# A chunked delta rule with chunks of 128 tokens in place of 64

## The chip, the cores and the metric

The kernel runs on one core of one Trainium2 chip. The time is that of the device, in microseconds (us), from the start of the program to its end. TensorE (PE in the profile) multiplies matrices, VectorE (DVE), ScalarE (ACT) and GpSimd (POOL) work element by element, SyncE (SP) issues transfers. The engines run their own instruction streams in order and meet at semaphores.

## What is computed

Two layers, one after the other, on a sequence of 1024 tokens of width 1024. The change lies in one part of the second layer, the gated delta rule with 4 heads of width 128. The reference computes it by chunks; here CHUNK is 64 and dk = dv = 128:

```python
gc = jnp.cumsum(g.reshape(b, h, n, CHUNK), axis=-1)
diff = gc[..., :, None] - gc[..., None, :]
decay = jnp.exp(jnp.where(tril_incl, diff, -jnp.inf))
kb = kc * bc[..., None]
a_mat = jnp.where(tril_strict, jnp.einsum('bhnid,bhnjd->bhnij', kb, kc) * decay, 0.0)
l_mat = a_mat + jnp.eye(CHUNK)
u = triangular_solve(l_mat, vc * bc[..., None])
w = triangular_solve(l_mat, kb * jnp.exp(gc)[..., None])
attn_intra = jnp.einsum('bhnid,bhnjd->bhnij', qc, kc) * decay
...
def step(state, inp):                       # scanned over the chunks
    v_new = u_i - w_i @ state
    o_i = qd_i @ state + a_i @ v_new
    state = state * gl_i + kt_i.T @ v_new
```

The recurrence S_t = exp(g_t)(I - beta_t k_t k_t^T) S_(t-1) + beta_t k_t v_t^T does not depend on how the tokens are cut into chunks, so a kernel may choose another chunk.

## The kernel before, in words

The kernel is a row of stages, each with its own block of instructions and a barrier behind it. The stage in question is `stage_delta` (L1559), between the projections of the second layer and `stage_causal`. Its input (q, k and v, turned, for all tokens) lies in SBUF already. Only the gate's constants and three masks are loaded.

The 1024 tokens are 8 tiles of 128. All 4 heads are done in one step: a step of TensorE is 4 matmuls of 128 columns (the trace counts 8 records, two for each float32 matmul; transposes have one) into one PSUM bank of 512 columns, and VectorE, ScalarE or GpSimd then handle 128x512 elements in one instruction. Three things are done for each tile:

- **front** (L1644): decays, the gram matrix of k, the product with q, the matrix A = strict lower part of the gram matrix times the decays, and the first level of the inverse, T (and X, its transpose). With CHUNK 64 the masks `upper`, `strict` and `levels` leave two blocks of 64x64 in each 128x128 matrix.
- **inv** (L1696): the inverse of the unit triangle by doubling. Level l joins blocks of 2^l to blocks of 2^(l+1). A level is a fixed loop over three engines: `z` (TensorE, Z = Al X, L1708), a copy of Z from PSUM (ScalarE, L1984), `update` (TensorE, dX = T Z at L1719 and dT = Z T at L1723), then X - dX (L1862) and T - dT (L1865) on VectorE. The next `z` waits for both (L1702, L1703). The last level needs no dT. Level 0 is done in the front, levels 1 to 5 here. `apply` (L1727) then makes u and w.
- **rec** (L1738): the recurrence. `read` (L1740) multiplies w and q with the state S, VectorE makes v_new (L1880); `write` (L1757) makes the update of S and the product of attention and v_new; VectorE adds the update to the decayed state (L1887), which GpSimd has made (L2098). A chunk has one read and one write, a tile of 128 tokens has two of each, with 64 rows in them.

The order of all engines is written out by `order` (L1612). Round i runs the front of tile i, the inverse of tile i-1 and the recurrence of tile i-2, dovetailed by levels: between `z` and `update` of a level stands a piece of the front, and behind `update` of levels 1 to 4 stands a read or a write. Rounds 0 and 1 have no recurrence, round 0 no inverse, round 8 has no front, round 9 only the recurrence. Rounds 2 to 7 have all three.

Of the kernel before, what the change touches and what calls it, by code (L numbers as in the profile page):

```python
# [42 lines left out]

D_IN2 = 4104
DN_HEADS, DK = 4, 128
CHUNK = 64
Z2, BA2, AQ2, AK2, AV2, AG2 = 1536, 2048, 2056, 2568, 3080, 3592
ATT_HEADS = 8
DILATION = (1, 4, 16)
STEPS = (P, P, P)  # L50
LEVELS = 6
CW = 256


# [1504 lines left out]
def stage_delta(nc, g):  # L1559
# [7 lines left out]
    with ExitStack() as ctx:  # L1567
# [10 lines left out]
        tl = k.sb("d_tl", [P, 12])  # L1578
        etl = k.sb("d_etl", [P, 3, 12])
# [63 lines left out]
        def _(pe):  # L1643
# [93 lines left out]

            class rec:  # L1738
                @staticmethod
                def read(t, c):  # L1740

                    n = 2 * t + c
                    r = slice(c * CHUNK, (c + 1) * CHUNK)
                    pe.wait_ge(s["w_copied"], t + 1)
                    if n >= 1:
                        pe.wait_ge(s["S_ready"], n)
                    if c == 0 and t >= 1:
                        pe.wait_ge(s["oq_ready"], t)
                    for h in range(H4):
                        last = nc.tensor.matmul(bank(6)[r, h, :], wT[:, t % 2, h, r], S[:, h, :], start=True, stop=True)  # L1750
                    last.then_inc(s["wS_ready"], 1)
                    for h in range(H4):
                        last = nc.tensor.matmul(bank(7)[r, h, :], g.qT[:, h, t * P + c * CHUNK:t * P + (c + 1) * CHUNK],
                                                S[:, h, :], start=True, stop=True)

                @staticmethod
                def write(t, c):  # L1757

                    n = 2 * t + c
                    r = slice(c * CHUNK, (c + 1) * CHUNK)  # L1760
                    pe.wait_ge(s["vnew_ready"], n + 1)
                    if c == 0 and t >= 1:
# [23 lines left out]
        def _(dve):  # L1786
# [6 lines left out]
            class front:  # L1793
                @staticmethod
                def first(t):
                    dve.wait_ge(s["gcb_ready"], t + 1)
                    if t >= 1:
                        dve.wait_ge(s["decays_done"], t)
                    for h in range(H4):

                        nc.vector.tensor_scalar(dd[:, 0, h, :], bank(0)[:, h, :], gc[:, t, h:h + 1], 0.0,
                                                ALU.subtract, ALU.max)
                        nc.vector.tensor_scalar(dd[:, 1, h, :], bank(0)[:, h, :], gc[:, t, h:h + 1], 0.0,
                                                ALU.subtract, ALU.min)
                    for c in range(2):
                        r = slice(c * CHUNK, (c + 1) * CHUNK)
# [31 lines left out]
                @staticmethod  # L1838
                def attn(t):
                    dve.wait_ge(s["attn_ready"], t + 1)  # L1840
                    dve.wait_ge(s["decT_masked"], t + 1)
                    if t >= 3:
                        dve.wait_ge(s["av_ready"], 2 * (t - 2))
# [26 lines left out]

            class rec:
                @staticmethod
                def read(t, c):
                    n = 2 * t + c
                    r = slice(c * CHUNK, (c + 1) * CHUNK)
                    dve.wait_ge(s["wS_ready"], n + 1)
                    dve.wait_ge(s["u_copied"], t + 1)
                    if n >= 2:
                        dve.wait_ge(s["av_ready"], n - 1)
                    nc.vector.tensor_tensor(vnew[r, :, :], u[r, t % 2, :, :], bank(6)[r, :, :], ALU.subtract).then_inc(s["vnew_ready"], 1)  # L1880

                @staticmethod
                def write(t, c):
                    n = 2 * t + c
                    dve.wait_ge(s["dS_ready"], n + 1)
                    dve.wait_ge(s["Sg_ready"], n + 1)
                    nc.vector.tensor_tensor(S[:, :, :], Sg[:, :, :], bank(6), ALU.add).then_inc(s["S_ready"], 1)  # L1887

                @staticmethod
                def finish(t):  # L1890
                    dve.wait_ge(s["av_ready"], 2 * t + 2)
# [42 lines left out]
        def _(act):  # L1934
            class front:
                @staticmethod
                def first(t):
# [4 lines left out]
                        act.wait_ge(s["dec_masked"], t)  # L1942
                        act.wait_ge(s["decT_masked"], t)
                    if t >= 3:
                        act.wait_ge(s["Sg_ready"], 2 * (t - 2))
# [30 lines left out]
            class inv:  # L1976
# [13 lines left out]
                @staticmethod  # L1990
                def apply(t):
                    if t >= 2:
                        act.wait_ge(s["vnew_ready"], 2 * (t - 1))
                    act.wait_ge(s["u_ready"], t + 1)
                    nc.scalar.copy(u[:, t % 2, :, :], bank(3)).then_inc(s["u_copied"], 1)
                    if t >= 2:
                        act.wait_ge(s["wS_ready"], 2 * (t - 1))
                    act.wait_ge(s["w_ready"], t + 1)
                    nc.scalar.copy(wT[:, t % 2, :, :], bank(4)).then_inc(s["w_copied"], 1)

            class rec:
                @staticmethod
                def read(t, c):
                    pass

                @staticmethod
# [1 line left out]
                    pass  # L2008

                @staticmethod  # L2010
                def write(t, c):
# [15 lines left out]
        def _(pool):  # L2027
# [6 lines left out]
            class front:  # L2034
# [13 lines left out]
                def khat_turn(t):  # L2048
# [2 lines left out]
                        pool.wait_ge(s["w_ready"], t - 1)  # L2051
                    nc.gpsimd.tensor_tensor(kbe[:, t % 2, :, :], khat[:, :, :], per_row(be[:, t, :]), ALU.mult).then_inc(s["kbe_ready"], 1)
                    if t >= 3:
                        pool.wait_ge(s["dS_ready"], 2 * (t - 2))
# [34 lines left out]

            class rec:  # L2090
                @staticmethod
                def read(t, c):

                    n = 2 * t + c
                    if n >= 1:
                        pool.wait_ge(s["S_ready"], n)
                    decay = etl[:, t % 3, 4:12].rearrange("p (h c) -> p h c", c=2)[:, :, c]
# [3 lines left out]
                def write(t, c):  # L2101
                    if c == 0 and t >= 1:
                        square(t - 1)

                @staticmethod
# [645 lines left out]
```

## Time and profile before

| | us |
|---|---|
| median of 3 runs | 1763.53 (1762.84 to 1763.92) |
| profiled execution | 1763.42 |
| its span in the profile | 1761.6 |
| delta stage, first to last matmul | 1216.9 to 1480.0 |
| a round with front, inverse and recurrence | 29.90 |

The page gives each engine's busy time over the whole span. The stage is read from the rows in order of time, further below: each has the start, the time, the line and operation, the count of records, and in brackets how long the engine sat idle before and for whom. A time from one start to the next start holds the idle time too, and is what the sums go by.

### The profile page before, as it was taken

The page shows a single profiled execution, that of the slowest core. Times are in us where ns is not written, and L with a number is a line of the kernel's source. Part 1 is how long each engine was busy: PE and PEld are TensorE (multiplying, and loading weights), DVE is VectorE, ACT ScalarE, POOL GpSimd, SP SyncE. Part 2 cuts the span into 40 slices and gives each one's busy share as a digit, 9 for nine tenths or more (in the row PEclk, how much of TensorE's full clock was granted, in tenths as well). Part 3 has the DMA queues.
Part 4 walks back from the last instruction along what each step waited for, and adds up shares of the span by engine and source line. Part 5 has one row for each costly group of instructions (what it writes and reads, how often), then busy time and mean ns, then how long its engine had stood idle before and what let it go on. Part 6 is the DMA issues. An engine that isn't in the chain of part 4 may idle for free. (4 is left out here: it accounts for less than half of the span.)

```text
span 1761.6 us, 27770 instructions
## 1 busy us (share of the span) xinstructions
PE 1632.9 (93%) x11048; PEld 1465.0 (83%) x11048; DVE 887.5 (50%) x1668; ACT 598.5 (34%) x1171; POOL 449.3 (26%) x508
## 2 busy tenths in 40 slices
PE   6999999799997998899999999996899997899799
PEld 6998899678876997678999988895788886899687
DVE  5339100588886997244041544342455553677431
ACT  5231011377774563233221223232212111566300
POOL 0212211000003562330122222212555541332320
PEclk9999999899998999899999999998999998999899
DMA  7312112000002111652142552201000002211242
GB/s 223 67 58 87 47 55 73 20 1 1 1 1 79 55 37 29 184 165 85 24 50 73 94 68 55 48 29 34 1 1 1 1 1 90 67 49 37 74 143 73
DMA packets 78454, 100.33 MB, mean 57 GB/s; under 512 B 20559, under 2 KB 63311, under 8 KB 78328
## 3 DMA queue, kind: packets, MB, share of 16 engines
q1 hardware_dynamic: 78328, 98.57, 21.2%
q8 instruction: 89, 1.46, 0.3%
q14 instruction: 37, 0.30, 0.1%
HBM read 75.45 MB, written 23.11 MB: 56 GB/s over the span
## 5 line engine op out<-in xcount | busy, mean ns | idle before, releaser
L301 POOL TENSOR_TENSOR p_w_lo<-p_w_raw,p_w_hi 128x2048 fp32r<-128x2048 f32 (+1 forms) x27 | 126.9, 4699 | 554.1 <-ACT p_w_hi L296 554.1
L332 PE MATMUL op_ps<-p_w_hi,w_out_hi 128*128 128x256 f32 (+1 forms) x640 | 182.1, 284 | 0.4 <-ACT p_spill L357 0.4
L332 PE MATMUL op_ps<-p_w_hi,w_out_lo 128*128 128x256 f32 (+1 forms) x640 | 179.7, 281 | 0.0
L332 PE MATMUL op_ps<-p_w_lo,w_out_hi 128*128 128x256 f32 (+1 forms) x640 | 179.6, 281 | 0.0
L332 PE MATMUL p_ps<-p_w_hi,hT_hi 128*128 128x256 f32 x576 | 163.5, 284 | 0.0
L332 PE MATMUL p_ps<-p_w_lo,hT_hi 128*128 128x256 f32 x576 | 162.8, 283 | 0.0
L332 PE MATMUL p_ps<-p_w_hi,hT_lo 128*128 128x256 f32 x576 | 162.8, 283 | 0.0
L332 PEld LDWEIGHTS op_ps<-p_w_hi,w_out_hi 128*128 128x128 f32 x640 | 120.6, 188 | 1.5 <-ACT p_spill L357 0.8
L332 PEld LDWEIGHTS op_ps<-p_w_lo,w_out_hi 128*128 128x128 f32 x640 | 120.8, 189 | 0.0
L332 PEld LDWEIGHTS op_ps<-p_w_hi,w_out_lo 128*128 128x128 f32 x640 | 120.6, 188 | 0.0
L296 ACT CAST p_w_hi<-p_w_raw 128x2048 fp32r<-128x2048 f32 (+1 forms) x29 | 55.3, 1908 | 167.5 <-DMA p_w_raw<-w_in 89.0
L332 PEld LDWEIGHTS p_ps<-p_w_lo,hT_hi 128*128 128x128 f32 x576 | 109.3, 190 | 0.0
L332 PEld LDWEIGHTS p_ps<-p_w_hi,hT_hi 128*128 128x128 f32 x576 | 109.3, 190 | 0.0
L332 PEld LDWEIGHTS p_ps<-p_w_hi,hT_lo 128*128 128x128 f32 x576 | 109.2, 190 | 0.0
L746 DVE TENSOR_TENSOR a_pt_lo<-a_ps,a_pt_hi 128x512 fp32r<-128x512 f32 x128 | 82.3, 684 | 24.1 <-ACT a_pt_hi L806 24.1
L806 ACT CAST a_pt_hi<-a_ps 128x512 fp32r<-128x512 f32 x128 | 68.8, 590 | 54.6 <-PE a_ps L670 54.5
L741 DVE TENSOR_REDUCE a_stat<-a_ps 128x1 f32<-128x1024 f32 x64 | 77.7, 1214 | 2.2 <-PE a_ps L660 2.2
L2296 PE MATMUL c_ps<-c_v,c_prob_t 128*128 128x128 f32 x576 | 76.2, 279 | 0.0
L332 PE MATMUL op_ps<-w_out_hi,p_w_hi 128*128 128x512 f32 x192 | 76.1, 396 | 0.0
L941 PEld LDWEIGHTS b_ps<-b_v,b_prob_t 128*128 128x128 f32 x544 | 70.0, 191 | 7.2 <-issue 1.6
L332 PE MATMUL op_ps<-w_out_hi,p_w_lo 128*128 128x512 f32 x192 | 75.7, 394 | 0.0
L332 PE MATMUL op_ps<-w_out_lo,p_w_hi 128*128 128x512 f32 x192 | 75.5, 393 | 0.0
(291 smaller groups left out, 4063.4 us busy)
## 6 DMA issues: line engine op xcount, KB each, us to landing
p_w_raw<-w_in SPq DMA_DIRECT2D x28, 1024.0 KB, 8.3
s_gate<-p_spill SPq DMA_DIRECT2D x48, 128.0 KB, 1.8
kbT<-x SPq DMA_DIRECT2D x8, 512.0 KB, 5.9
b_w_raw<-w_out SPq DMA_DIRECT2D x8, 512.0 KB, 5.4
qT<-s_gate SPq DMA_DIRECT2D x8, 512.0 KB, 5.5
qT<-x SPq DMA_DIRECT2D x8, 512.0 KB, 3.6
s_x<-qT SPq DMA_DIRECT2D x8, 512.0 KB, 2.6
c_table<-s_line SPq DMA_DIRECT2D x8, 512.0 KB, 4.0
```

What stands on the lines that cost most here:

```text
L296: self.nc.scalar.copy(self.w_hi[:, c % 2, :, 0:w], self.raw[:, :, 0:w]).then_inc(self.w_hi_ready, 1)
L301: ops.tensor_tensor(self.w_lo[:, c % 2, :, 0:w], self.raw[:, :, 0:w], self.w_hi[:, c % 2, :, 0:w].bitcast(F32), ALU.subtract).then_inc(sel ...
L332: last = self.nc.tensor.matmul(out, lhs, rhs, start=(kt == 0 and i == 0), stop=(kt == KT - 1 and i == 2))
L741: nc.vector.tensor_reduce(stat[:, 0, u:u + 1], s, AX.X, ALU.max, negate=True).then_inc(max_ready, 1)
L746: nc.vector.tensor_tensor(part(pt_lo, grp, half, i), ps[:, 4 + half, :].rearrange("p (c q) -> p c q", c=4), part(pt_hi, grp, half, i).bitc ...
L806: nc.scalar.copy(part(pt_hi, grp, half, i), ps[:, 4 + half, :].rearrange("p (c q) -> p c q", c=4)).then_inc(pt_hi_ready, 1)
L941: last = nc.tensor.matmul(ps[:, 6 + u % 2, 0:P], prob_t[:, u % 2, j * P:(j + 1) * P], v[:, t0 + j, p * P:(p + 1) * P], start=(j == 0), sto ...
L2296: last = nc.tensor.matmul(ps[:, 6 + u % 2, 0:P], prob_t[:, u % 3, j * P:(j + 1) * P], v[:, j, pair * P:(pair + 1) * P], start=(j == 0), st ...
```

## The change

`CHUNK` becomes 128 and `LEVELS` 7. A tile is one chunk: its triangle is a full 128x128 one, which takes a level more, and there is one read and one write of the state for a tile. The read stands behind level 2 and the write behind level 4. The recurrence's matmuls have 128 rows in place of 64. The end-of-chunk decays `tl` are one column for each head, which makes one small VectorE instruction less for each tile.

```diff
-CHUNK = 64
+CHUNK = 128
-LEVELS = 6
+LEVELS = 7
...
@@ order
-                if f and l >= 2:
+                if f and 2 <= l <= 5:
                     (front.khat_turn, front.gram, front.attn, front.x0)[l - 2](i)
                 if v:
                     inv.update(i - 1, l)
                 if f and l == 1:
                     front.khat(i)
-                if r and l <= 4:
-                    (rec.read, rec.write)[(l - 1) % 2](i - 2, (l - 1) // 2)
+                if r and l == 2:
+                    rec.read(i - 2)
+                if r and l == 4:
+                    rec.write(i - 2)
...
@@ tensor, rec
                     for h in range(H4):
-                        last = nc.tensor.matmul(bank(6)[r, h, :], wT[:, t % 2, h, r], S[:, h, :], start=True, stop=True)
+                        last = nc.tensor.matmul(bank(6)[:, h, :], wT[:, t % 2, h, :], S[:, h, :], start=True, stop=True)
...
-                        last = nc.tensor.matmul(bank(6)[:, h, :], ktail[r, t % 3, h, :], vnew[r, h, :], start=True, stop=True)
+                        last = nc.tensor.matmul(bank(6)[:, h, :], ktail[:, t % 3, h, :], vnew[:, h, :], start=True, stop=True)
...
-                        last = nc.tensor.matmul(bank(5)[r, h, :], attnT[r, t % 3, h, r], vnew[r, h, :], start=True, stop=True)
+                        last = nc.tensor.matmul(bank(5)[:, h, :], attnT[:, t % 3, h, :], vnew[:, h, :], start=True, stop=True)
...
@@ vector, front.first
-                    for c in range(2):
-                        r = slice(c * CHUNK, (c + 1) * CHUNK)
-                        nc.vector.tensor_tensor(tl[r, 0:H4], bank(0)[r, :, (c + 1) * CHUNK - 1], gc[r, t, :], ALU.subtract)
-                    ends = bank(0).rearrange("p h (c j) -> p h c j", c=2)[:, :, :, CHUNK - 1]
-                    nc.vector.tensor_copy(tl[:, 4:12].rearrange("p (h c) -> p h c", c=2), ends).then_inc(s["diffs_done"], 1)
+                    nc.vector.tensor_tensor(tl[:, 0:H4], bank(0)[:, :, CHUNK - 1], gc[:, t, :], ALU.subtract)
+                    nc.vector.tensor_copy(tl[:, H4:2 * H4], bank(0)[:, :, CHUNK - 1]).then_inc(s["diffs_done"], 1)
```

The other lines of the diff carry the same through: waits that counted 2 t + c count t, slices `[r, ...]` become whole tiles, the masks come out of `CHUNK` and `LEVELS`.

TensorE in a round with all three parts, before, from the `update` of level 1 on. L1719 and L1723 are the update, L1708 is z, L1750/L1753 the read, L1765/L1768 the write, L1670 a transpose of the front.

```order
L1719 MATMUL d_ps<-d_Z,d_T 128x128 x4
L1723 MATMUL d_ps<-d_T,d_Z 128x128 x4
L1750 MATMUL d_ps<-d_S,d_wT 64x128 x4
L1753 MATMUL d_ps<-d_S,qT 64x128 x4
L1708 MATMUL d_ps<-d_X,d_Al 128x128 x4
L1670 MATMUL d_ps<-ident,d_khat 128x128 x4
L1719 MATMUL d_ps<-d_Z,d_T 128x128 x4
L1723 MATMUL d_ps<-d_T,d_Z 128x128 x4
L1765 MATMUL d_ps<-d_vnew,d_ktail 128x128 x4
L1768 MATMUL d_ps<-d_vnew,d_attnT 64x128 x4
```

The same place after the change (L1721 and L1725 are the update, L1710 z, L1749/L1752 the read, L1672 and L1680 pieces of the front):

```order
L1721 MATMUL d_ps<-d_Z,d_T 128x128 x4
L1725 MATMUL d_ps<-d_T,d_Z 128x128 x4
L1710 MATMUL d_ps<-d_X,d_Al 128x128 x4
L1672 MATMUL d_ps<-ident,d_khat 128x128 x4
L1721 MATMUL d_ps<-d_Z,d_T 128x128 x4
L1725 MATMUL d_ps<-d_T,d_Z 128x128 x4
L1749 MATMUL d_ps<-d_S,d_wT 128x128 x4
L1752 MATMUL d_ps<-d_S,qT 128x128 x4
L1710 MATMUL d_ps<-d_X,d_Al 128x128 x4
L1680 MATMUL d_ps<-d_khatT 128x128 x4
```

Behind the update of level 1 z now follows directly; the read stands behind the update of level 2, with 128x128 outputs, and behind the update of level 3 z follows directly again.

TensorE at the end of the inverse, before, from z of level 5 on (L1693 is a transpose of the front, L1732/L1735 are `apply`):

```order
L1708 MATMUL d_ps<-d_X,d_Al 128x128 x4
L1693 MATMUL d_ps<-ident,d_T 128x128 x4
L1719 MATMUL d_ps<-d_Z,d_T 128x128 x4
L1732 MATMUL d_ps<-d_vb,d_X 128x128 x4
L1735 MATMUL d_ps<-d_X,d_kbe 128x128 x4
L1708 MATMUL d_ps<-d_X,d_Al 128x128 x4
```

and after (L1695 is that transpose, L1734/L1737 are `apply`):

```order
L1710 MATMUL d_ps<-d_X,d_Al 128x128 x4
L1695 MATMUL d_ps<-ident,d_T 128x128 x4
L1721 MATMUL d_ps<-d_Z,d_T 128x128 x4
L1725 MATMUL d_ps<-d_T,d_Z 128x128 x4
L1710 MATMUL d_ps<-d_X,d_Al 128x128 x4
L1721 MATMUL d_ps<-d_Z,d_T 128x128 x4
L1734 MATMUL d_ps<-d_vb,d_X 128x128 x4
L1737 MATMUL d_ps<-d_X,d_kbe 128x128 x4
L1710 MATMUL d_ps<-d_X,d_Al 128x128 x4
```

The update of level 5 now has its second half, and a z and a first half of an update, level 6, come behind it with nothing in between.

## Rows read from the trace of the kernel before

**Rows 1.** Busy time by stretch: stretch, length, engines, PEclk, DMA share, GB/s.
```profile
1352.50:1382.40 29.90, 28.61 (x232) 26.36 (x233) 16.48 (x32) 6.33 (x12) 16.40 (x14) 1.00 0.00 1
...
1232.00:1236.00 4.00, 2.64 (x11) 2.24 (x12) 0.63 (x1) 0.58 (x1) 4.00 (x4) 0.51 0.00 2
...
1248.00:1253.00 5.00, 4.02 (x36) 3.86 (x36) 2.07 (x3) 0.59 (x1) 2.88 (x3) 1.00 0.02 3
```

**Rows 2.** TensorE in order of time, repeating tile: start, us, line, operation, count, idle before.
```profile
1336.92 1.10 PE L1719 MATMUL d_ps<-d_Z,d_T 128*128 128x128 f32 x8
...
1340.73 1.16 PE L1708 MATMUL d_ps<-d_X,d_Al 128*128 128x128 f32 x8
...
1342.62 1.10 PE L1719 MATMUL d_ps<-d_Z,d_T 128*128 128x128 f32 x8
...
1344.55 1.16 PE L1765 MATMUL d_ps<-d_vnew,d_ktail 64*128 64x128 f32 x8
...
1346.65 1.16 PE L1708 MATMUL d_ps<-d_X,d_Al 128*128 128x128 f32 x8
...
1348.48 1.16 PE L1719 MATMUL d_ps<-d_Z,d_T 128*128 128x128 f32 x8 [0.24 <-ACT d_Z L1984]
1350.42 1.16 PE L1732 MATMUL d_ps<-d_vb,d_X 128*128 128x128 f32 x8 [0.78 <-DVE d_X L1862]
...
1352.51 1.13 PE L1708 MATMUL d_ps<-d_X,d_Al 128*128 128x128 f32 x8
...
1355.24 1.06 PE L1719 MATMUL d_ps<-d_Z,d_T 128*128 128x128 f32 x8
...
1357.12 1.09 PE L1750 MATMUL d_ps<-d_S,d_wT 128*64 128x128 f32 x8
...
1359.02 1.16 PE L1708 MATMUL d_ps<-d_X,d_Al 128*128 128x128 f32 x8
...
1412.31 1.13 PE L1708 MATMUL d_ps<-d_X,d_Al 128*128 128x128 f32 x8
```

**Rows 3.** TensorE in order of time, before and in the first tile's inverse.
```profile
1216.93 0.61 PE L1778 MATMUL d_ps<-d_g,d_upper 128*128 128x32 f32 x2 [10.02 <-DVE d_g L1920]
...
1244.25 1.16 PE L1719 MATMUL d_ps<-d_Z,d_T 128*128 128x128 f32 x8 [0.24 <-ACT d_Z L1984]
...
1247.29 1.13 PE L1708 MATMUL d_ps<-d_X,d_Al 128*128 128x128 f32 x8 [0.98 <-DVE d_T L1865]
...
1249.15 1.10 PE L1719 MATMUL d_ps<-d_Z,d_T 128*128 128x128 f32 x8
...
1252.13 1.13 PE L1708 MATMUL d_ps<-d_X,d_Al 128*128 128x128 f32 x8 [0.98 <-DVE d_T L1865]
```

**Rows 4.** VectorE in order of time, first tile and then repeating tile.
```profile
1246.34 0.69 DVE L1865 TENSOR_TENSOR d_T<-d_T,d_ps 128x512 f32<-128x512 f32 x1 [0.20 <-PE d_ps L1723]
...
1356.65 0.32 DVE L1807 TENSOR_TENSOR d_tl<-d_ps,d_gc 64x4 f32<-64x4 f32 x2
1356.98 0.17 DVE L1809 COPY d_tl<-d_ps 128x8 f32<-128x8 f32 x1
...
1357.79 0.68 DVE L1865 TENSOR_TENSOR d_T<-d_T,d_ps 128x512 f32<-128x512 f32 x1
```

**Rows 5.** TensorE in order of time, last inverse and last recurrence.
```profile
1442.21 1.13 PE L1708 MATMUL d_ps<-d_X,d_Al 128*128 128x128 f32 x8
1444.02 1.16 PE L1719 MATMUL d_ps<-d_Z,d_T 128*128 128x128 f32 x8 [0.68 <-ACT d_Z L1984]
...
1447.89 1.16 PE L1708 MATMUL d_ps<-d_X,d_Al 128*128 128x128 f32 x8
...
1471.98 1.09 PE L1750 MATMUL d_ps<-d_S,d_wT 128*64 128x128 f32 x8 [0.73 <-ACT d_wT L1999]
...
1475.97 1.09 PE L1750 MATMUL d_ps<-d_S,d_wT 128*64 128x128 f32 x8
```

**Rows 6.** DMA issues at the stage's start: KB each, us to landing.
```profile
d_levels<-c_levels SPq DMA_DIRECT2D x1, 384.0 KB, 3.2
```

More of the change, by code:

```diff
@@ L1577, in stage_delta @@
         dec = k.sb("d_dec", [P, 2, H4, P])
-        tl = k.sb("d_tl", [P, 12])
-        etl = k.sb("d_etl", [P, 3, 12])
+        tl = k.sb("d_tl", [P, 8])
+        etl = k.sb("d_etl", [P, 3, 8])
         khat = k.sb("d_khat", [P, H4, P])
@@ L1739, in read, with write @@
                 @staticmethod
-                def read(t, c):
-                    n = 2 * t + c
-                    r = slice(c * CHUNK, (c + 1) * CHUNK)
+                def read(t):
                     pe.wait_ge(s["w_copied"], t + 1)
-                    if n >= 1:
-                        pe.wait_ge(s["S_ready"], n)
-                    if c == 0 and t >= 1:
+                    if t >= 1:
+                        pe.wait_ge(s["S_ready"], t)
                         pe.wait_ge(s["oq_ready"], t)
                     for h in range(H4):
-                        last = nc.tensor.matmul(bank(6)[r, h, :], wT[:, t % 2, h, r], S[:, h, :], start=True, stop=True)
+                        last = nc.tensor.matmul(bank(6)[:, h, :], wT[:, t % 2, h, :], S[:, h, :], start=True, stop=True)
                     last.then_inc(s["wS_ready"], 1)
                     for h in range(H4):
-                        last = nc.tensor.matmul(bank(7)[r, h, :], g.qT[:, h, t * P + c * CHUNK:t * P + (c + 1) * CHUNK],
+                        last = nc.tensor.matmul(bank(7)[:, h, :], g.qT[:, h, t * P:(t + 1) * P],
                                                 S[:, h, :], start=True, stop=True)
                 @staticmethod
[L1757 to L1762, printed above, removed]
+                def write(t):
+                    pe.wait_ge(s["vnew_ready"], t + 1)
+                    if t >= 1:
                         pe.wait_ge(s["o_ready"], t)
                     for h in range(H4):
-                        last = nc.tensor.matmul(bank(6)[:, h, :], ktail[r, t % 3, h, :], vnew[r, h, :], start=True, stop=True)
+                        last = nc.tensor.matmul(bank(6)[:, h, :], ktail[:, t % 3, h, :], vnew[:, h, :], start=True, stop=True)
                     last.then_inc(s["dS_ready"], 1)
                     for h in range(H4):
-                        last = nc.tensor.matmul(bank(5)[r, h, :], attnT[r, t % 3, h, r], vnew[r, h, :], start=True, stop=True)
+                        last = nc.tensor.matmul(bank(5)[:, h, :], attnT[:, t % 3, h, :], vnew[:, h, :], start=True, stop=True)
                     last.then_inc(s["av_ready"], 1)
@@ L1842, in attn @@
                     if t >= 3:
-                        dve.wait_ge(s["av_ready"], 2 * (t - 2))
+                        dve.wait_ge(s["av_ready"], t - 2)
                     nc.vector.tensor_tensor(attnT[:, t % 3, :, :], bank(0), dec[:, 1, :, :], ALU.mult).then_inc(s["attnT_ready"], 1)
@@ L1872, in read, with write @@
                 @staticmethod
[L1873 to L1876, printed above, removed]
+                def read(t):
+                    dve.wait_ge(s["wS_ready"], t + 1)
                     dve.wait_ge(s["u_copied"], t + 1)
-                    if n >= 2:
-                        dve.wait_ge(s["av_ready"], n - 1)
-                    nc.vector.tensor_tensor(vnew[r, :, :], u[r, t % 2, :, :], bank(6)[r, :, :], ALU.subtract).then_inc(s["vnew_ready"], 1)
+                    if t >= 1:
+                        dve.wait_ge(s["av_ready"], t)
+                    nc.vector.tensor_tensor(vnew[:, :, :], u[:, t % 2, :, :], bank(6), ALU.subtract).then_inc(s["vnew_ready"], 1)
                 @staticmethod
[L1883 to L1886, printed above, removed]
+                def write(t):
+                    dve.wait_ge(s["dS_ready"], t + 1)
+                    dve.wait_ge(s["Sg_ready"], t + 1)
                     nc.vector.tensor_tensor(S[:, :, :], Sg[:, :, :], bank(6), ALU.add).then_inc(s["S_ready"], 1)
@@ L1890, in finish @@
                 def finish(t):
-                    dve.wait_ge(s["av_ready"], 2 * t + 2)
+                    dve.wait_ge(s["av_ready"], t + 1)
                     if t >= 1:
@@ L1944, in first @@
                     if t >= 3:
-                        act.wait_ge(s["Sg_ready"], 2 * (t - 2))
+                        act.wait_ge(s["Sg_ready"], t - 2)
                     nc.scalar.activation(dec[:, 0, :, :], dd[:, 0, :, :], ACT.Exp, scale=-1.0)
@@ L1992, in apply @@
                     if t >= 2:
-                        act.wait_ge(s["vnew_ready"], 2 * (t - 1))
+                        act.wait_ge(s["vnew_ready"], t - 1)
                     act.wait_ge(s["u_ready"], t + 1)
@@ L1996, in apply @@
                     if t >= 2:
-                        act.wait_ge(s["wS_ready"], 2 * (t - 1))
+                        act.wait_ge(s["wS_ready"], t - 1)
                     act.wait_ge(s["w_ready"], t + 1)
@@ L2002, in read @@
                 @staticmethod
-                def read(t, c):
+                def read(t):
                     pass
@@ L2010, in write @@
                 @staticmethod
-                def write(t, c):
+                def write(t):
                     pass
@@ L2091, in read, with write @@
                 @staticmethod
[L2092 to L2097, printed above, removed]
+                def read(t):
+                    if t >= 1:
+                        pool.wait_ge(s["S_ready"], t)
+                    decay = etl[:, t % 3, H4:2 * H4]
                     nc.gpsimd.tensor_tensor(Sg[:, :, :], S[:, :, :], per_row(decay), ALU.mult).then_inc(s["Sg_ready"], 1)
                 @staticmethod
-                def write(t, c):
-                    if c == 0 and t >= 1:
+                def write(t):
+                    if t >= 1:
                         square(t - 1)
```

3 lines of the change are left out of this document (1 added, 2 removed).

## The prediction

> **What bounds the kernel now.** I read the busy times by stretch first. In a repeating stretch of the delta stage, 29.90 us long, TensorE is busy 28.61 us, VectorE 16.48, GpSimd 16.40 and ScalarE 6.33, at a granted clock of 1.00 [rows 1]. So TensorE sets the pace there, and the others have over 13 us to spare in each round. Next I read TensorE in order of time. z of level 1 starts at 1352.51 and, two rounds later, at 1412.31, which is twice 29.90: the rounds repeat [rows 2]. The reader should see in these rows that TensorE hardly waits (0.24 and 0.78 us where a bracket stands), although each level is a loop over three engines. It doesn't wait because other work lies in the two places of a level where it could: a piece of the front between z and the update, a read or write of the state between the update and the next z.
>
> That cover is what I ask about, because the change takes half of it away. Two stretches show a level without it. In round 1, which has no recurrence, z starts 0.98 us after TensorE fell idle, waiting for T of VectorE [rows 3]. In round 8, which has no front, the update waits 0.68 us for the copy of Z [rows 5]. I count from start to start, since such a distance holds work and wait together.
>
> **What a covered and a bare turn take.** From the start of an update to the start of the next z:
> - with a read behind it: 1355.24 to 1359.02, 3.78 us, and 1336.92 to 1340.73, 3.81 [rows 2]
> - with a write behind it: 1342.62 to 1346.65, 4.03 [rows 2]
> - bare: 1249.15 to 1252.13, 2.98, and 1244.25 to 1247.29, 3.04 [rows 3]
>
> So a read or write of about 2 us that is taken out gives only 0.8 to 1.0 us. The rest of it was cover.
>
> **Round with all three parts (6 of them, rounds 2 to 7).**
> - Level 1: the read goes. z of level 2 then waits for T. VectorE first has the decay differences and the small `tl` instructions in its queue, so T starts at 1357.79 and ends at 1358.47 [rows 4]. The change has one L1807 less (two took 0.32), so T ends 0.16 earlier, at 1358.31. From the end of T (1246.34 + 0.69 = 1247.03 [rows 4]) to z (1247.29 [rows 3]) are 0.26 us, so z starts at 1358.57, that is 3.33 after the update in place of 3.78: -0.45.
> - Level 2: a write goes, the read comes in. The write takes 2.10 (1344.55 to 1346.65), a read with 64 rows 1.90 (1357.12 to 1359.02) [rows 2]. A read or write with 128 rows stands in no row. The nearest thing is an update, two steps of full width: 1.88 (1355.24 to 1357.12) and 1.93 (1342.62 to 1344.55) [rows 2]. I take 1.90, with 1.88 and 2.10 as ends: -0.20.
> - Level 3: the read goes, bare turn: 3.81 to 2.98, -0.83.
> - Level 4: the write stays, with 128 rows: 2.10 to 1.90, -0.20.
> - Level 5: was the last level, and its update led to `apply` 1.94 us later (1348.48 to 1350.42 [rows 2]). That distance now belongs to level 6. In its place comes an update with both halves and a bare turn: +3.04.
> - Level 6: z and a bare wait for the copy of Z: 1442.21 to 1444.02, +1.81 [rows 5].
>
> Sum: -1.68 + 4.85 = +3.17 us for a round, 29.90 to 33.07. Six rounds: +19.0.
>
> The Trainium skill, in TensorEngine Tiling (Array Packing), section Key Properties, says that changing the tiling mode drains TensorE; by that the 64-row matmuls cost twice, once on the way in and once on the way out, and the change would gain where they go. The trace has 0.20 us more for a write than for a read, which may be such a drain, and none at a read, which at 1.90 equals a full-width pair [rows 2]. If the rule charged reads too, the read that stays would be 0.20 shorter in each tile, 1.6 us in all, and the sum 1784 in place of 1785.7.
>
> **The other rounds.** Round 1 has no recurrence to take out: +4.85 for the level, -0.16 for `tl`: +4.7. Round 8 has no front: level 1 was 3.87 with its read (1444.02 to 1447.89 [rows 5]) and becomes a bare turn of 3.04, -0.83; level 3 the same; levels 2 and 4 -0.20 each; the new level +4.85: +2.8. Round 9 is recurrence alone, where nothing was cover: one read and one write go, 1471.98 to 1475.97, -3.99 [rows 5], and the write that stays is -0.20: -4.2. Round 0: the smaller `tl` stands ahead of the chain, -0.2.
>
> **What costs nothing, and what hides it.** GpSimd makes one mask product more for a tile and one decayed state less, both 128x512, with 13.5 us idle in a round [rows 1]. The masks are made a round before they are used. Its one decayed state now stands behind `read` at level 2, ahead of the masks, and VectorE wants it only at level 4. The square of the outputs moves behind the masks, and VectorE sums it at the round's end. VectorE has one X and one T more and one v_new and one S less for a tile; X, T and v_new of level 2 fall in its idle time. ScalarE has one more copy of Z, in its idle 23 us. The mask load grows from 384 to 448 KB, from 3.2 us [rows 6] to some 3.7 by size; TensorE waits until 1216.93 for the gates anyway, 10.02 us long [rows 3], so 0, and 0.5 at most. The read of a tile needs the state of the tile before, which is written a round earlier in both kernels.
>
> **Sum.** 19.0 + 4.7 + 2.8 - 4.2 - 0.2 = +22.1 us, for which the levels pay 8 x 4.85 = 38.8 and the recurrence gives back 16.7. The profiled execution took 1763.42 (span 1761.6), 0.1 below the median of 1763.53. So 1785.6, and 1785.7 against the median.
>
> Ends: 16 reads and writes at 1.88 in place of 1.90 give -0.3, at 2.10 +3.2. All bare turns at 2.98, level 1 too, give 6 x 0.35 + 8 x 0.06 + 2 x 0.06, -2.7. All at 3.33 give 6 x 0.35 + 8 x 0.29 + 2 x 0.29, +5.0. With the masks' 0.5 the forecast's own range is 1782.7 to 1794.4.
>
> **Rivals.**
> 1. *TensorE's work decides, and the turns are covered after all* (faster). Counted in steps the change is good: of a round with all parts it takes a read and a write (1.90 + 2.10) and 0.20 from the write that stays, and adds three steps (z, half an update at level 5, half an update at level 6) of 0.95, half of 1.90, 2.9 in all: -1.3. Rounds 2 to 8 -9.1, round 1 +2.9, round 9 -4.2: -10.4, or 1753. For it: 28.61 busy of 29.90, so the stage looks bound by TensorE's busy time [rows 1]. Against it: the bare turns, which show where time goes when the cover goes [rows 3, 5]; nothing else stands in TensorE's queue to fill them, since the order is fixed. It decides if a turn without cover costs under a third of what these rows have: +22.1 is -10.4 plus 32.5 us of new waits. Chance 6 in 100.
> 2. *The clock falls in the new waits* (much slower). The head of the stage, after long waits, ran at 0.51, that is 1.2 GHz [rows 1]. A round's 28.6 us of busy TensorE would take up to as much again: with one round so it is 1814, with all eight near 2000. Against it: the stretch 1248 to 1253, with the same bare turns and TensorE busy 4.02 of 5.00, has 1.00, that is 2.4 GHz [rows 1]. The new rounds are denser than that. The Trainium skill, in TensorE: Matmul & The Clock Gate, section Loop structure matters more than you think, warns that waits between matmuls let the engine go cold; what it would do here is this rival, and the trace bears it out for the long waits at the stage's head alone. Chance 4 in 100.
> 3. *Half and half*: the reads and writes of full width are cheaper than any pair in the rows, or round 1 misleads because its VectorE has less to do, so that the sum comes out within 3 us of nothing. I see no row for it. Chance 3 in 100.
>
> **How the numbers follow.** The forecast has 87 in 100, its time is 1785.7. I take the range from 1780 to 1796, a little wider than its ends, since the stage behind starts at another moment, with a clock still low. A difference of 0.2% (3.5 us) is about what a measurement can tell from none. Slower 91 in 100 (forecast and rival 2), same 3, faster 6.
>
> **What would show it.** In the changed profile a repeating round is 33.1 us, not 29.9. TensorE waits for T behind levels 1, 3 and 5 (about 1.4, 1.0 and 1.0 us) and for Z at level 6 (0.7), and not behind 2 and 4. A read and a write with 128 rows take 1.9 each. The recurrence alone at the end takes about 3.8 in place of 8. PEclk stays 1.00. A round under 30 us would prove me wrong, as would a clock under 1.00 in rounds 2 to 8.

## The result and the profile after

The changed kernel took 1784.49 us (median of 4 runs, 1782.26 to 1787.65) against 1763.72 for the kernel before, measured beside it: a ratio of 1.0117, 95% interval 1.0099 to 1.0136. Five more runs later gave 1781.89 against 1766.25, 1.0088 (1.0072 to 1.0104). So it is slower by 16 to 21 us; the forecast was 22.

The profiled execution took 1782.26. From the first matmul of round 0's front to the last matmul of the recurrence the delta stage has 262.2 us before and 280.6 after, +18.4; all the rest has 1501.2 and 1501.7. In what follows "the stage" is that stretch, since the rest varied between 1498.8 and 1506.8 us over the fourteen profiles of this study, in kernels that don't differ there: more than most of the effects looked for.

First TensorE in order of time in round 2 of the changed kernel (the columns of [rows 2]; L1710 is z, L1721 the start of an update, L1749 the read, L1762 the write, L1734 `apply`):

```profile
1267.25 1.13 PE L1710 MATMUL d_ps<-d_X,d_Al 128*128 128x128 f32 x8
...
1269.98 1.06 PE L1721 MATMUL d_ps<-d_Z,d_T 128*128 128x128 f32 x8
...
1273.05 1.13 PE L1710 MATMUL d_ps<-d_X,d_Al 128*128 128x128 f32 x8 [1.12 <-DVE d_T L1859]
...
1274.86 1.16 PE L1721 MATMUL d_ps<-d_Z,d_T 128*128 128x128 f32 x8 [0.24 <-ACT d_Z L1975]
...
1276.75 1.06 PE L1749 MATMUL d_ps<-d_S,d_wT 128*128 128x128 f32 x8
...
1278.53 1.06 PE L1710 MATMUL d_ps<-d_X,d_Al 128*128 128x128 f32 x8
...
1280.32 1.10 PE L1721 MATMUL d_ps<-d_Z,d_T 128*128 128x128 f32 x8
...
1283.30 1.13 PE L1710 MATMUL d_ps<-d_X,d_Al 128*128 128x128 f32 x8 [0.98 <-DVE d_T L1859]
...
1285.16 1.10 PE L1721 MATMUL d_ps<-d_Z,d_T 128*128 128x128 f32 x8
...
1286.99 1.06 PE L1762 MATMUL d_ps<-d_vnew,d_ktail 128*128 128x128 f32 x8
...
1288.78 1.06 PE L1710 MATMUL d_ps<-d_X,d_Al 128*128 128x128 f32 x8
...
1290.51 1.16 PE L1721 MATMUL d_ps<-d_Z,d_T 128*128 128x128 f32 x8 [0.24 <-ACT d_Z L1975]
...
1293.55 1.13 PE L1710 MATMUL d_ps<-d_X,d_Al 128*128 128x128 f32 x8 [0.98 <-DVE d_T L1859]
1295.35 1.16 PE L1721 MATMUL d_ps<-d_Z,d_T 128*128 128x128 f32 x8 [0.68 <-ACT d_Z L1975]
1297.29 1.16 PE L1734 MATMUL d_ps<-d_vb,d_X 128*128 128x128 f32 x8 [0.78 <-DVE d_X L1856]
...
1299.33 0.91 PE L1710 MATMUL d_ps<-d_X,d_Al 128*128 128x128 f32 x6
```

Two things are to be seen. The brackets: TensorE waits for T (L1859) at the z behind levels 1, 3 and 5, 1.12, 0.98 and 0.98 us, for Z at level 6 0.68, and not at all behind levels 2 and 4, where the read and the write stand. In the kernel before [rows 2] there was no wait for T. And the distances from update to z: 3.07, 3.67, 2.98, 3.62 and 3.04 at levels 1 to 5. The round is 32.08 (1267.25 to 1299.33), 32.13 in the rounds behind it.

VectorE at level 1 of the next round, to be laid beside [rows 4]:

```profile
1303.46 0.15 DVE L1802 TENSOR_TENSOR d_tl<-d_ps,d_gc 128x4 f32<-128x4 f32 x1
1303.53 0.15 DVE L1803 COPY d_tl<-d_ps 128x4 f32<-128x4 f32 x1
1303.60 0.68 DVE L1856 TENSOR_TENSOR d_X<-d_X,d_ps 128x512 f32<-128x512 f32 x1
1304.19 0.68 DVE L1859 TENSOR_TENSOR d_T<-d_T,d_ps 128x512 f32<-128x512 f32 x1
```

The two small `tl` instructions now start 0.07 us apart, where 64-row ones had 0.33 between the first two and the third.

The recurrence alone in round 9, which answers to the last two of [rows 5]:

```profile
1494.41 1.16 PE L1749 MATMUL d_ps<-d_S,d_wT 128*128 128x128 f32 x8 [0.73 <-ACT d_wT L1990]
...
1496.35 1.16 PE L1762 MATMUL d_ps<-d_vnew,d_ktail 128*128 128x128 f32 x8
1497.34 1.06 PE L1765 MATMUL d_ps<-d_vnew,d_attnT 128*128 128x128 f32 x8
```

From 1494.41 to 1498.40 are 3.99 us; before, from 1471.98 to the end of the last matmul at 1480.02, 8.04.

Last, the busy times by stretch (columns of [rows 1]; a round is counted here from the step behind z of level 1): first a plain round, then the round from 1364.6 to 1399.2, then the 3 us before its clock fell and the stretch at the lower clock:

```profile
1332.42:1364.56 32.14, 27.08 (x227) 25.58 (x226) 16.07 (x31) 6.91 (x13) 16.62 (x14) 1.00 0.00 1
1364.56:1399.23 34.67, 29.65 (x227) 28.21 (x226) 16.06 (x31) 6.91 (x13) 16.61 (x14) 0.90 0.00 1
1389.18:1392.18 3.00, 1.62 (x12) 1.46 (x13) 0.45 (x1) 0.58 (x1) 0.00 (x0) 1.00 0.00 0
1392.18:1399.01 6.83, 6.05 (x29) 5.75 (x29) 2.57 (x4) 1.17 (x2) 0.00 (x0) 0.50 0.01 2
```

A plain round has TensorE busy 27.08 of 32.14 us, where it was 28.6 of 29.9 [rows 1]: less work and more time. The next round is 34.67 us long. Its PEclk is 0.90: behind the bare levels 5 and 6 the clock stands at 0.50, 1.2 GHz, for 6.83 us, which costs 2.5 us. In the 3 us ahead of that TensorE was busy 1.62. The stage's +18.4 is thus +15.9 and one such dip.

### The profile page after: what moved, and what is told of

Read it like the earlier page. It is cut to its first block and busy times, and to the rows that moved or that the text cites. A ratio compares the mean times of both kernels' runs of the same rounds, so it can differ in the third digit from the quotient of the medians.

```text
span 1780.5 us, 27642 instructions
## 1 busy us (share of the span) xinstructions
PE 1623.6 (91%) x10984; PEld 1461.8 (82%) x10984; DVE 881.7 (50%) x1660; ACT 602.8 (34%) x1179; POOL 452.9 (25%) x508
## 5 line engine op out<-in xcount | busy, mean ns | idle before, releaser
L1975 ACT COPY d_Z<-d_ps 128x512 f32<-128x512 f32 x48 | 28.1, 585 | 157.4 <-PE d_ps L1710 157.4
L1710 PE MATMUL d_ps<-d_X,d_Al 128*128 128x128 f32 x384 | 54.7, 287 | 27.4 <-DVE d_T L1859 26.5
```

The source lines that it names most:

```text
L1710: last = nc.tensor.matmul(bank(3)[:, h, :], Al[:, t % 2, l, h, :], X[:, t % 2, h, :], start=True, stop=True)
L1975: nc.scalar.copy(Z[:, :, :], bank(3)).then_inc(s["Z_copied"], 1)
```

## The experiments

All runs are compared in two ways: by the ratio to the kernel before, measured beside them on the same chip, and by the rounds in the profile. Three of the kernels (the recurrence alone, full rows, six levels) compute something else and serve to price a part.

**The level alone.** The kernel before with `LEVELS = 7` and chunks of 64:

```diff
-LEVELS = 6
+LEVELS = 7
...
-                if f and l >= 2:
+                if f and 2 <= l <= 5:
```

> The kernel before (chunks of 64, two reads and two writes for a tile) with a seventh level. In chunks of 64 that level's mask selects only zeros, so the inverse is the same and only the work is added. Cover theory: each of 8 tiles pays a full update and a bare turn (3.04 us) and a bare wait for Z (1.81 us), 4.85, so 1763.5 + 38.8 = 1802.3. Rival, only TensorE's steps count: three steps of 0.95 for a tile, 1763.5 + 22.8 = 1786.3.

Measured: 1811.2 us (1808.9 to 1813.3), 1.0263 (1.0246 to 1.0280). The round that the forecast was about:

```profile
1309.00:1343.74 34.74, 31.79 (x259) 29.19 (x258) 17.85 (x34) 6.92 (x13) 17.63 (x15) 1.00 0.00 1
1378.40:1415.70 37.30, 34.35 (x258) 31.82 (x258) 17.85 (x34) 6.92 (x13) 17.62 (x15) 0.91 0.00 1
```

A plain round is 34.74, 4.84 over the 29.90 before: the level costs what the cover theory says, not 2.85. The stage has 306.1, +43.9; the second row (37.30, PEclk 0.91) and the last stretch (PEclk 0.96) are 2.6 and 2.5 us longer by a dip of the clock each, and without the two it is +38.8, the number forecast. The dips (5.1) and a rest of the kernel that was 5.4 us longer (1506.6) make the difference between 1802 and 1811.

**The recurrence alone.** The changed kernel with `LEVELS = 6`: the level that joins the two halves of a tile is left out.

> The changed kernel with six levels: the last level of the inverse is left out (the two halves of a tile are not joined), all else is as changed. Cover theory with the prediction's own terms: 1763.5 - 16.7 = 1746.8. With the widths that the changed kernel's trace shows (a covered turn with a 128-row read or write 3.58, level 1 bare 3.07): a round of 27.2 in place of 29.9, six times -2.7, round 8 -2.8, round 9 -4.0, rounds 0 and 1 -0.8, so 1739.7. Rival, that the recurrence was only cover: nothing comes back but round 9, 1759.5.

Measured: 1740.98 us (1740.1 to 1745.4), 0.9873 (0.9857 to 0.9889).

```profile
1321.70:1349.00 27.30, 23.89 (x202) 22.74 (x202) 14.71 (x29) 6.33 (x12) 15.39 (x13) 1.00 0.01 2
```

Rounds of 27.3, stage 238.9, -23.3. This is the second set of numbers, not the prediction's 16.7: the recurrence gives back 7 us more than forecast. Both parts together are -23.3 + 38.8 = +15.5, against +15.9 in the changed kernel without its dip: they add up.

**Full rows in the kernel before.** Where do the 7 us come from? In the kernel before, every matmul of the recurrence on 128 rows:

```diff
-                        last = nc.tensor.matmul(bank(6)[r, h, :], wT[:, t % 2, h, r], S[:, h, :], start=True, stop=True)
+                        last = nc.tensor.matmul(bank(6)[:, h, :], wT[:, t % 2, h, :], S[:, h, :], start=True, stop=True)
...
-                        last = nc.tensor.matmul(bank(6)[:, h, :], ktail[r, t % 3, h, :], vnew[r, h, :], start=True, stop=True)
+                        last = nc.tensor.matmul(bank(6)[:, h, :], ktail[:, t % 3, h, :], vnew[:, h, :], start=True, stop=True)
```

and so the other two; a memset of `vnew` ahead of all.

> The kernel before, with each matmul of the recurrence on all 128 rows in place of 64, same count, same places, same waits; the values of the recurrence are wrong by it (both halves of a tile are used at once). Theory that a 64-row matmul costs more than a 128-row one, since it changes how the array is divided: a turn with a read goes from 3.8 to 3.6 with 0.1 more at the z behind it (together -0.3), one with a write -0.5, so -1.6 for each of rounds 2 to 8, -11, 1752.5. Rival, that rows don't matter and the shorter steps in the changed kernel come from their place in the order: 1763.5.

Measured: 1756.73 us (1754.7 to 1759.0), 0.9958 (0.9943 to 0.9972); stage 250.9, -11.3; rounds of 28.28.

```profile
1327.94 1.06 PE L1750 MATMUL d_ps<-d_S,d_wT 128*128 128x128 f32 x8
...
1329.72 1.06 PE L1708 MATMUL d_ps<-d_X,d_Al 128*128 128x128 f32 x8
...
1333.34 1.06 PE L1765 MATMUL d_ps<-d_vnew,d_ktail 128*128 128x128 f32 x8
...
1335.13 1.06 PE L1708 MATMUL d_ps<-d_X,d_Al 128*128 128x128 f32 x8
1336.02 1.06 PE L1678 MATMUL d_ps<-d_khatT 128*128 128x128 f32 x8
```

Twice the rows, and the kernel is faster by 0.4%. The stage gave the 11 us of the theory; the median fell by 8.2, with a rest of the kernel that was longer in the profile (1506.8). A read takes 1.78 (1327.94 to 1329.72) where it took 1.90, a write 1.79 where it took 2.10, and z behind it 0.89 (1335.13 to 1336.02). Two reads and two writes with 64 rows cost 1.6 us more in a round than with 128.

The single records of TensorE say where. In the kernel before they follow each other by 0.109 us within a 64-row step and by 0.112 within a full one, so the 64-row step itself is no slower. But from the last record of one shape to the first of another it is 0.20, and from that one to the next 0.16 or 0.21: full to 64 rows ahead of the read (1357.12), 64 to full behind it (1359.02). Between the two steps of a read, which have one shape (128\*64), it is 0.109. A write has a third change between its own steps (64\*128, then 64\*64), which is why it costs more. By these gaps a read loses 0.30 and a write 0.51, for two of each 1.62: the whole 29.90 - 28.28. With full rows the records at these places follow each other by 0.11 us. What costs is the change of shape.

**Z in another bank.** The changed kernel; z of an even level no longer waits for T, which was a wait for bank 3.

```diff
+                    if m >= 1 and l % 2:
                         pe.wait_ge(s["T_ready"], (LEVELS - 2) * t + l - 1)
+                    if l in (2, 6) and t >= 1:
+                        pe.wait_ge(s["S_ready"], t - 1 if l == 2 else t)
+                    if l == 4 and t >= 1:
+                        pe.wait_ge(s["vnew_ready"], t)
...
-                        last = nc.tensor.matmul(bank(3)[:, h, :], Al[:, t % 2, l, h, :], X[:, t % 2, h, :],
+                        last = nc.tensor.matmul(bank(3 if l % 2 else 6)[:, h, :], Al[:, t % 2, l, h, :], X[:, t % 2, h, :],
```

The update of an even level waits for T instead, and ScalarE copies Z from bank 6 there.

> The changed kernel, with Z of levels 2, 4 and 6 in PSUM bank 6, which the recurrence leaves free then, so that z waits for X alone and the wait for T moves to the update. Theory that the bare turn is the wait for bank 3 and T: z starts 0.6 us earlier at level 2 and 0.9 at levels 4 and 6, 2.4 for each of 8 tiles, 1784.5 - 19 = 1765.5. Rival, that z could not start earlier (X is as late, or the update's own wait for T then takes its place): 1784.5.

Measured: 1758.07 us (1753.4 to 1762.6), 0.9961 (0.9944 to 0.9978) against the kernel before; stage 254.6, rounds of 29.28.

```profile
1303.43 1.10 PE L1728 MATMUL d_ps<-d_Z,d_T 128*128 128x128 f32 x8
...
1305.36 1.13 PE L1715 MATMUL d_ps<-d_X,d_Al 128*128 128x128 f32 x8
...
1312.57 1.16 PE L1728 MATMUL d_ps<-d_Z,d_T 128*128 128x128 f32 x8 [0.24 <-ACT d_Z L1982]
...
1314.55 1.13 PE L1715 MATMUL d_ps<-d_X,d_Al 128*128 128x128 f32 x8
```

The bare turns of levels 3 and 5 are 1.93 and 1.98 in place of 2.98 and 3.04: nothing is left in them but the update's two steps. Level 1 has 2.32 in place of 3.07; in round 8, where VectorE has no decay differences ahead of X, it has 1.98. That is -2.86 for a round, a little more than the 2.4 forecast, since z follows without any gap and not 0.15 us later. It is 3.7 us of the 7.4 by which the forecast of 1765.5 was too long; the clock did not dip in this stage, 2.5 more. The wait in a bare turn was for the bank, since z needs X but not T; a cover hides it and another bank removes it. With it the changed kernel is 0.4% faster than the kernel before, and its stage 7.6 us shorter.

**The recurrence spread over four turns.** One step behind each of levels 1 to 4 in place of two behind levels 2 and 4.

```diff
-                if r and l == 2:
-                    rec.read(i - 2)
-                if r and l == 4:
-                    rec.write(i - 2)
+                if r:
+                    if l == 1:
+                        rec.read(i - 2)
+                    if l == 2:
+                        rec.read_q(i - 2)
+                    if l == 3:
+                        rec.write(i - 2)
+                    if l == 4:
+                        rec.write_o(i - 2)
```

> The changed kernel with read and write cut into their two steps, one behind each of the updates of levels 1 to 4 (state times w, state times q, write, output), in place of two at level 2 and two at level 4. One step of 0.9 us fits into the wait of about 1.0 us of a turn. Cover theory: turns 1 to 4 all take 3.0 to 3.1, the two of 3.58 lose 0.5 each, so -1.1 in rounds 2 to 8, 1784.5 - 7.7 = 1776.8. Rival, that the new waits of v_new on TensorE's next step eat it: 1784.

Measured: 1778.24 us (1774.6 to 1785.5), 1.0075 (1.0053 to 1.0098); stage 278.5 with a dip of the clock in its last part. By the time alone this is unclear against the 1781.89 of the changed kernel beside it (below). The rounds say more: rounds 2 and 4 have 31.08 and 31.03, as forecast, and rounds 3, 5, 6 and 7 have 32.10 to 32.11. VectorE in rounds 2, 3 and 4, at the first T (from SBUF only, no PSUM), and GpSimd beside it:

```profile
1285.51 0.82 DVE L1853 TENSOR_TENSOR d_T<-ident,d_Al 128x512 f32<-128x512 f32 x1
...
1316.59 1.82 DVE L1853 TENSOR_TENSOR d_T<-ident,d_Al 128x512 f32<-128x512 f32 x1
...
1348.72 0.68 DVE L1853 TENSOR_TENSOR d_T<-ident,d_Al 128x512 f32<-128x512 f32 x1
```

```profile
1280.83 9.09 POOL L2079 TENSOR_TENSOR d_Al<-d_A,d_levels 128x512 f32<-128x512 f32 x7 [1.15 <-DVE d_A L1843]
...
1313.14 1.04 POOL L2117 TENSOR_TENSOR d_osq<-vT 128x512 f32<-128x512 f32 x1
1314.14 7.84 POOL L2079 TENSOR_TENSOR d_Al<-d_A,d_levels 128x512 f32<-128x512 f32 x6
```

The same instruction takes 0.82, 1.82 and 0.68 us. In round 3 the square of the outputs (L2117) stands in the row of masks, and the following masks start at other moments than in round 2. The turn of level 4 grows by 1 us, from 3.08 to 4.08. By the single records T waits for a GpSimd instruction that runs and ends 0.59 us after the next one starts: in round 2 the next mask starts 0.23 after T (0.82), in round 3 a mask starts 0.01 after T, T waits it out, and the next starts 1.23 after T (1.82). In round 4 a mask again starts 0.01 after T, and this time the mask waits: T takes 0.68 and the mask 1.80 in place of 1.27. Which of the two wins such a tie the runs don't say.

**The square behind the masks.** The spread kernel with that instruction moved behind the last mask.

> The spread kernel with one GpSimd instruction moved: the square of the outputs stands behind the six masks in place of ahead of them. In the spread kernel's trace, rounds 3, 5, 6 and 7 are 1 us longer than rounds 2 and 4, and in them the first T (VectorE, from SBUF alone) took 1.73 to 1.82 us in place of 0.68 to 0.82, while GpSimd began the masks at another moment. If its duration hangs on how the two engines' instructions meet, T takes the same 0.7 to 0.9 in all of rounds 2 to 7, all are 31.1, and the kernel is 4 us below the spread one. Rival, that the long rounds have another cause: they stay.

Measured: 1777.36 us (1775.3 to 1780.1), 1.0067 (1.0047 to 1.0088); rounds 2 to 6 are 31.10 to 31.21, the stage is 273.5, 5.0 less. The four long rounds give 3.9 of it. The rest is the clock, which dips here at the end of round 7 for 6.83 us and in the spread kernel's round 8 for 10.24.

```profile
1321.11 0.80 DVE L1853 TENSOR_TENSOR d_T<-ident,d_Al 128x512 f32<-128x512 f32 x1
```

In rounds 1 to 7 this instruction has 0.80 to 0.84, and the next mask starts 0.22 to 0.25 us after it. So the long rounds came from how it met GpSimd's. The median did not follow the stage: 0.9 us down, not 4. The rest of the kernel took 1506.7 in this profile and 1501.0 in the spread one, and the stages' difference goes under in that.

**Filled waits.** The changed kernel with useless matmuls in the bare waits of levels 5 and 6 (a gram matrix into a bank already read).

```diff
...
+                if f and l == LEVELS - 1:
+                    front.fill(i)
                 if v:
                     inv.update(i - 1, l)
+                if f and l == LEVELS - 2:
+                    front.fill(i)
...
```

> The changed kernel with two steps of matmuls more in rounds 1 to 7 (the gram matrix again, into a bank that nobody reads any more): one behind the update of level 5, one between z and the update of level 6. They fill the two bare waits and lengthen the chain by 0.2 us at level 6 and nothing at level 5, +1.4 in all. If the half-clock stretches come from the low activity there, there are none in rounds 1 to 7, PEclk is 1.00 in all of them, and the median is the same or 1 to 2 us lower than the changed kernel's, with less spread. Rival, that the stretches have another cause: they stay, and the time is 1.4 us up.

> The changed kernel again, unedited, as the control of the three beside it. Its profile had one stretch of 6.8 us at half clock in the delta stage, which cost 2.7 us. If such a stretch comes by chance where the turns are bare, the runs spread from 1781 (none) to 1788 (three), and this profile has another number of them, perhaps at another place.

> The filler kernel once more. If the filled waits hold the clock, PEclk is 1.00 in rounds 1 to 7 again, and these rounds are 32.1 to 32.3 us; else one of them has a stretch of half clock and is 34.6.

> The changed kernel, unedited, a third time: with bare turns at levels 5 and 6, one stretch of half clock of 6 to 7 us somewhere in rounds 2 to 8, as in the two profiles before, one round or the stage's end 2.5 us longer by it.

Measured: filler 1781.19 us (median of 6 runs, 1778.0 to 1784.1), 1.0085 (1.0070 to 1.0100); changed kernel 1781.89 (median of 5, 1779.3 to 1784.4), 1.0088 (1.0072 to 1.0104). One more run of each later gave 1780.68 and 1783.59. In two profiles the filler kernel has PEclk 1.00 in all rounds from 1 on and stages of 278.6 and 279.2. In three profiles the changed kernel has one dip each (round 5 twice, once behind the last front, with stages of 280.6, 280.3 and 280.6). Two stretches of the filler kernel and of the changed kernel's third profile:

```profile
1364.00:1396.20 32.20, 28.64 (x240) 27.33 (x240) 16.12 (x32) 6.92 (x13) 16.63 (x14) 1.00 0.00 1
1396.20:1428.30 32.10, 28.64 (x240) 27.33 (x240) 16.05 (x32) 6.91 (x13) 16.62 (x14) 1.00 0.00 1
```

```profile
1366.90:1401.57 34.67, 29.65 (x226) 28.20 (x225) 16.07 (x32) 6.91 (x13) 16.61 (x14) 0.90 0.00 1
```

The fill also runs in round 0, which I had not counted; it makes that round 1.3 to 2.2 longer and round 1, whose clock it holds, 1.0 shorter. The clock's part is as expected: two steps of work that nobody needs add at most 0.2 us to a round, and the dip is gone. The forecast of 1.4 us for a longer chain did not come: z to update of level 6 is 1.86 in place of 1.80, and update to `apply` 1.88 in place of 1.94. The clock's part is small: 2.5 us in 280. The time can't tell the two kernels apart. Nor does the number of dips explain the spread of the runs: without dips in its profiles the filler kernel spreads over 6 us, the changed kernel over 5.

**Everything covered.** What the runs pointed to: chunks of 128, with each wait covered by one step or taken away.

```diff
+        ZB = {1: 3, 2: 6, 3: 5, 4: 6, 5: 5, 6: 6}
...
+            inside = {1: ("gcb",), 2: ("turn",), 3: ("read",), 4: ("gram",), 5: ("write",), 6: ("attn",)}
+            behind = {1: ("decays",), 2: ("exps", "khat_turn"), 4: ("read_q", "t0"), 5: ("x0",), 6: ("write_o",)}
             for l in range(1, LEVELS):
-                if v and l >= 2:
+                if v:
                     inv.z(i - 1, l)
+                for part in inside[l]:
...
                 if v:
                     inv.update(i - 1, l)
...
+                for part in behind.get(l, ()):
...
```

The parts of `inside` stand between z and the update of a level, those of `behind` after the update, and ZB is the bank of Z. `gcb`, `turn`, `decays`, `exps` and `t0` are pieces of what the front did in larger ones. `decays` on VectorE now stands behind X and T of level 1.

> Chunks of 128, with Z of levels 2 to 6 in banks 6 and 5 (z waits for X alone), X and T of level 1 ahead of the decay differences on VectorE, and the front and the recurrence cut into steps of 0.9 us, one between z and the update of each level. TensorE's own steps of a round are 19 of the inverse, 3 and 4 half ones of the front, 4 of the recurrence, 25.2 us. Theory that a round is then TensorE's steps plus little: 26 us, and the kernel at 1727, within 8. Rival, that the loop over three engines still bounds it: 29 us a round, 1755.

Measured: 1733.38 us (1730.0 to 1737.6), 0.9817 (0.9798 to 0.9836). It beats both kernels. The stage has 230.8 us. The forecast was 1727, within 8, from a round of 26.

```profile
1317.27:1343.55 26.28, 26.24 (x227) 25.58 (x225) 16.61 (x31) 7.10 (x13) 16.59 (x14) 1.00 0.01 2
```

```profile
1318.16 1.10 PE L1737 MATMUL d_ps<-d_Z,d_T 128*128 128x128 f32 x8
...
1320.10 1.13 PE L1724 MATMUL d_ps<-d_X,d_Al 128*128 128x128 f32 x8
...
1326.25 1.10 PE L1737 MATMUL d_ps<-d_Z,d_T 128*128 128x128 f32 x8
...
1328.18 1.13 PE L1724 MATMUL d_ps<-d_X,d_Al 128*128 128x128 f32 x8
...
1334.55 1.10 PE L1737 MATMUL d_ps<-d_Z,d_T 128*128 128x128 f32 x8
...
1336.38 0.60 PE L1704 MATMUL d_ps<-ident,d_T 128*128 128x128 f32 x4
1336.82 1.06 PE L1724 MATMUL d_ps<-d_X,d_Al 128*128 128x128 f32 x8
```

A round is 26.28 us. No bracket stands behind any of its rows: update to z is 1.94 and 1.93 at levels 1 and 3, and at level 5 1.83 to the start of `x0` (L1704).

**The same with six levels.**

> The kernel with everything covered, with six levels: the last level of the inverse is left out (the two halves of a tile are not joined), and its cover (the product with q, the output step) moves into and behind level 5. What a level costs where it is covered: theory, three of TensorE's steps, 2.8 us, so a round of 23.5 in place of 26.3 and 1733.4 - 22 = 1711. Rival, the 4.85 us of the bare kernel, a round of 21.4 and 1733.4 - 39 = 1694.

Measured: 1708.62 us (1707.3 to 1709.5), 0.9676 (0.9655 to 0.9696); rounds of 23.36, stage 206.5; the forecast was 1711 and 23.5.

```profile
1306.59:1329.97 23.38, 23.31 (x202) 22.73 (x201) 15.25 (x29) 6.53 (x12) 15.39 (x13) 1.00 0.01 2
```

26.28 - 23.36 = 2.92: covered, a level costs three steps, and bare 4.84. This kernel leaves out the joining of the halves too, so only its distance to the one above says something.

## Why the prediction was right, and where its sizes were off

- *What bounds the stage.* Right: TensorE's fixed order with a loop over three engines in it. The waits stand where the prediction put them, with 0.98 and 0.68 us as read from the uncovered stretches of the kernel before [rows 3, 5].
- *The new level, +4.85.* Right: 4.84 alone, and 3.04 and 1.80 in the changed kernel.
- *Bare turn at level 3, 2.98.* Right to the hundredth. At level 1 it is 3.07, forecast 3.33, with a wait of 1.12 and not 1.4. The step "one L1807 less, so T ends 0.16 earlier" was too small: from the first `tl` to X are 0.14 us, where from the first to the end of the last there were 0.50 [rows 4].
- *Read and write, 1.90 each.* Too much: 1.78 and 1.79. I took the pair that an update makes [rows 2], without seeing that its second step stood ahead of a 64-row one and was slow by it. In the kernel with full rows the update ahead of a read takes 1.79. The turns of levels 2 and 4 are 3.67 and 3.62 where my terms gave 3.88 and 3.83 (4.08 and 4.03 less 0.20), and from z to update behind them there are 1.79 and 1.73 where there were 1.89 and 1.83 [rows 2]: 0.62 in a round. With the 0.26 of level 1 that is 0.88 of the 0.94 us by which the forecast round, 33.07, was too long.
- *Sum.* Forecast +22.1 in the stage, found +15.9 without the dip. Six rounds are +13.4 (32.13 against 29.90) and not 19.0, which is nearly all of it. With the dip it is +18.4, and the time came out at 1784.5, 1.2 from the forecast, because a dip and the rest of the kernel leant the other way. That closeness is luck; the rounds are the test.
- *The Trainium skill on the tiling mode.* The prediction gave it 1.6 us, "if the rule charged reads too". It does more than that: full rows in the kernel before gave 11.3 us, 1.6 in each round. The prediction's "none at a read" was a misreading: the full-width pair it compared with was itself slowed by the read behind it. The Trainium skill, in TensorEngine Tiling (Array Packing), section Key Properties, says that a change of tiling mode drains TensorE; the trace agrees, with gaps of 0.20 and then 0.16 or 0.21 us between records at each change of shape, where 0.11 is usual in steps of either height.
- *Rival 1, work alone decides.* Wrong here: the level alone costs 4.84 for a tile, where its steps are under 3. But in the covered kernel it holds: a level costs its three steps.
- *Rival 2, the clock.* True in a small way. It had 4 chances in 100 for a whole round; what came is one stretch of 7 us at 1.2 GHz in each of three profiles, 2.5 us. The prediction named "a clock under 1.00 in rounds 2 to 8" as a sign of error, and it appeared. The stretch it argued from (1248 to 1253, at 1.00) had none. The dips, those of the level alone and of the two spread kernels too, all begin behind levels 5 and 6, where bare waits follow each other. All six profiles of kernels with these waits have one or two from round 2 on, and the other eight, where the waits are filled, gone or not there, have none before the end of the stage. The Trainium skill, in TensorE: Matmul & The Clock Gate, section Loop structure matters more than you think, shows a loop that loses the clock by a long DMA wait ahead of each matmul; here the trace shows the loss with waits of 1 us. What decides in which round it falls stays open: round 2 of the changed kernel has the same bare levels, with TensorE busy 1.34 of 3 us there (1292.5 to 1295.5), and kept 1.00.
- *Half and half*, a sum within 3 us of nothing, did not come.

## What to carry to other kernels

When an order interleaves two chains, what taking work out gives back is its duration less the wait that it covered, and the wait can be read where the pipeline fills or drains: there the same steps run without cover. Judge a change by the length of a repeating round, not by the total, when other stages vary by more. And ask what a wait is for: here the wait of 1 us behind an update was for a PSUM bank, not for data, and two more banks for Z with one step of cover for each gap turned a change that lost 1% into a kernel that gains 1.8%.

## What had not been expected

- Matmul steps with 64 rows cost more than with 128: a pair 1.90 or 2.10 us against 1.78, and the whole kernel takes 1756.7 with twice the rows, where it took 1764.9 beside it. It is the change between 64 and 128 rows that costs, 0.14 to 0.19 us each time.
- A VectorE instruction on 128x512 with both operands in SBUF took 0.68, 0.82, 0.97, 1.17, 1.27, 1.38 or 1.82 us in these traces, by how it met GpSimd's instructions; moving one GpSimd instruction brought it to 0.80 to 0.84 and rounds 3, 5 and 6 from 32.1 to 31.1 or 31.2. The Trainium skill, in SBUF — State Buffer, section SBUF: two separate sides, has one pair of SBUF ports for GpSimd and those VectorE instructions that read two SBUF operands, held by one of them for the whole instruction; the trace agrees: VectorE lost up to 1.14 us beside GpSimd instructions of 1.04 to 1.3, and where VectorE came first, the GpSimd instruction took 1.71 to 1.80 in place of 1.27.
- The clock fell to 1.2 GHz for 7 us with TensorE busy 1.47 to 1.62 of the 3 us just before, in each of three profiles of the changed kernel and in none of two with filler matmuls in its waits.
